# Delta-rule chunks of a gated delta net: four heads in flight with two PSUM banks each, levels confined to half of the columns, and one set of four tiles for scratch and levels

## The reference, cut to what matters

```python
k_beta = k * beta[..., None]
a_strict = jnp.where(idx[:, None] > idx[None, :],
                     jnp.einsum('bhncd,bhnsd->bhncs', k_beta, k) * decay, 0.0)
tri = a_strict + jnp.eye(c, dtype=jnp.float32)
u = lax.linalg.triangular_solve(tri, v * beta[..., None], left_side=True, lower=True, unit_diagonal=True)
w = lax.linalg.triangular_solve(tri, k_beta * jnp.exp(gc)[..., None], left_side=True, lower=True,
                                unit_diagonal=True)
qk = jnp.einsum('bhncd,bhnsd->bhncs', q, k) * decay
q_dec = q * jnp.exp(gc)[..., None]
k_dec = k * jnp.exp(g_last - gc)[..., None]
```

## Time and profile before

| what | value |
|---|---|
| median of 3 runs | 2913.43 us (2912.21 to 2916.68) |
| profiled execution | 2917.37 us, span 2915.6 us |
| mean granted clock in it | 0.92 |
| PE busy in the span | 2500.4 us (86%) |
| `stage_gdn_chunks`, first weight load to end of the last copy | 274.17 to 540.82 us |

### The profile page before, as it was taken

The page is one execution under the profiler, slowest core; times in us unless marked ns, Lnnn a source line. Parts: engine busy times, 40 slices in busy tenths (PEclk is TensorE's granted clock), DMA queues, the critical chain, the costliest instruction groups (busy, mean ns, idle before and its releaser), DMA issues. The chain is left out here.

```text
span 2915.6 us, 34741 instructions
## 1 busy us (share of the span) xinstructions
PE 2500.4 (86%) x13054; PEld 1953.1 (67%) x13054; DVE 1265.9 (43%) x2608; ACT 978.3 (34%) x1577; POOL 742.8 (25%) x204
## 2 busy tenths in 40 slices
PE   6996788877995696899799388979999888989998
PEld 4773777756773485567677265857887746768886
DVE  3533555445545323776554536143222453243122
ACT  2333111223552111673455225152322333343222
POOL 2430000042343231001334220413543301324441
PEclk8997889977997796999899698999999999999999
DMA  4251000015885233111688331213432302223321
GB/s 107 90 209 41 1 1 1 30 45 168 277 281 184 65 101 118 64 39 45 218 282 280 131 90 38 94 54 96 131 100 72 109 27 66 81 84 102 103 85 65
DMA packets 225098, 304.41 MB, mean 104 GB/s; under 512 B 52304, under 2 KB 139872, under 8 KB 224944
## 3 DMA queue, kind: packets, MB, share of 16 engines
q1 hardware_dynamic: 222656, 294.16, 31.3%
q0 software_dynamic: 2304, 8.39, 0.8%
HBM read 270.95 MB, written 31.56 MB: 104 GB/s over the span
## 5 line engine op out<-in xcount | busy, mean ns | idle before, releaser
L159 POOL TENSOR_TENSOR branch_weights_wl<-branch_weights_wf,branch_weights_wh 128x2048 fp32r<-128x2048 f32 (+1 forms) x66 | 303.9, 4604 | 770.2 <-ACT branch_weights_wh L153 770.2
L153 ACT ACTIVATE branch_weights_wh<-branch_weights_wf 128x2048 fp32r<-128x2048 f32 (+1 forms) x66 | 125.0, 1895 | 405.8 <-PE bprojc_acc L201 133.0
L201 PE MATMUL merge_acc<-xh,branch_weights_wh 128*128 128x512 f32 x384 | 151.4, 394 | 2.9 <-PEq L72 2.9
L201 PE MATMUL merge_acc<-xh,branch_weights_wl 128*128 128x512 f32 x384 | 150.3, 391 | 0.0
L201 PE MATMUL merge_acc<-xl,branch_weights_wh 128*128 128x512 f32 x384 | 149.5, 389 | 0.0
L159 POOL TENSOR_TENSOR nsa_weights_wl<-nsa_weights_wf,nsa_weights_wh 128x2048 fp32r<-128x2048 f32 x13 | 59.7, 4594 | 275.3 <-ACT nsa_weights_wh L153 275.3
L1556 PE MATMUL exp_ps_y<-rt_wf,exp_ht 128*128 128x512 f32 x256 | 117.2, 601 | 3.9 <-ACT exp_ht L1600 3.9
L1410 POOL TENSOR_TENSOR rt_wl<-rt_wf,rt_wh 128x2048 fp32r<-128x2048 f32 x16 | 82.6, 5163 | 128.9 <-ACT rt_wh L1406 128.9
L159 POOL TENSOR_TENSOR in_weights_wl<-in_weights_wf,in_weights_wh 128x2048 fp32r<-128x2048 f32 x16 | 75.3, 4709 | 129.1 <-ACT in_weights_wh L153 110.6
L201 PE MATMUL gproj_acc<-xh,in_weights_wh 128*128 128x512 f32 x256 | 100.8, 394 | 3.7 <-POOL in_weights_wl L159 3.7
L201 PE MATMUL gproj_acc<-xh,in_weights_wl 128*128 128x512 f32 x256 | 100.5, 393 | 0.0
(11 more groups left out here) (612 smaller groups left out, 6705.0 us busy)
## 6 DMA issues: line engine op xcount, KB each, us to landing
branch_weights_wf<-w_in SPq DMA_DIRECT2D x56, 1024.0 KB, 5.0
rt_wf<-moe_w_down SPq DMA_DIRECT2D x32, 1024.0 KB, 5.5
in_weights_wf<-gdn_w_in SPq DMA_DIRECT2D x16, 1024.0 KB, 5.6
rt_wf<-moe_w_gate SPq DMA_DIRECT2D x32, 512.0 KB, 7.4
rt_wf<-moe_w_up SPq DMA_DIRECT2D x32, 512.0 KB, 8.2
moe_rows<-rt_y SPq DMA_DIRECT2D x64, 256.0 KB, 2.1
moe_rows<-gproj_zeros SPq DMA_DIRECT2D x1, 12288.0 KB, 35.7
merge_bwf<-w_branch SPq DMA_DIRECT2D x12, 1024.0 KB, 5.0
```

The source lines that it names most:

```text
L153: act.activation(self.h[u][:, :, 0:self.cols(b)], self.s.f[u][:, :, 0:self.cols(b)], ACT.Copy).then_inc(self.s.hi_ready, 1)
L159: pool.tensor_tensor(self.l[u][:, :, 0:self.cols(b)], self.s.f[u][:, :, 0:self.cols(b)], self.h[u][:, :, 0:self.cols(b)].bitcast(F32), ALU ...
L201: mm = pe.matmul(self.acc[:, s, 0:cols], lhs[:, P * s:P * s + P], rhs, start=(u == 0 and k == 0 and n == 0), stop=(u == 1 and k == HALF - ...
```

## The change

`NB` is 4: two rounds of four heads. A head has two PSUM banks in place of four, and four SBUF tiles (`at`, `x`, `tm`, `um`) in place of ten, each used for several things in turn. The masks of levels 1 to 6 are transposed, so that the mask is laid on the product instead of on `at`. In a level only the half of the columns that can be nonzero is computed: `off` takes half of the columns of `tm` (64 of 128 per chunk, in runs of the block size) and writes them into the same half of the bank, DVE multiplies the whole bank with the mask into `x`, and `grow` makes two products of 64 columns, `um` with half of `x` and `x` with half of `um`, written side by side in bank 1. DVE subtracts these 256 columns each from the matching halves of `tm` and `um`. ACT's copy in the level is gone. Turning of keys and values moves from the start of a round to behind the levels, and with it its scaling; there ACT does both scalings and copies out the new keys.

```diff
+    NB, L = 4, LEVELS - 1
-        NB = 2
-        B = [{x: st.sb(f"{x}{i}", [P, TT, P]) for x in
-              ("dec", "decb", "eg", "at", "m", "x", "tm", "um", "kbg", "vb")} for i in range(NB)]
-        ps = [st.ps(f"ps{i}", 4) for i in range(NB)]
+        B = [{x: st.sb(f"{x}{i}", [P, TT, P]) for x in ("at", "x", "tm", "um")} for i in range(NB)]
+        ps = [st.ps(f"ps{i}", 2) for i in range(NB)]
...
+        def halves(ap, lv, e):
+
+            return ap.rearrange("p (b e s) -> p b e s", e=2, s=1 << lv)[:, :, e, :]
...
+                def off(i, r, lv):
+
+                    dve_did.wait(pe, i, r, "lower" if lv == 1 else f"lower{lv - 1}")
                     for c in range(TT):
+                        mm = pe.matmul(halves(bank(i, 0, c), lv, 0), B[i]["at"][:, c, :], halves(B[i]["tm"][:, c, :], lv, 0),
                                        start=True, stop=True)
...
+                def grow(i, r, lv):
...
+                    dve_did.wait(pe, i, r, f"off{lv}")
+                    if lv < L:
+                        for c in range(TT):
+                            pe.matmul(compact(ps[i][:, 1, 64 * c:64 * c + 64], lv), b["um"][:, c, :],
+                                      halves(b["x"][:, c, :], lv, 0), start=True, stop=True)
...
+                        mm = pe.matmul(compact(ps[i][:, 1, 256 + 64 * c:256 + 64 * c + 64], lv), b["x"][:, c, :],
+                                       halves(b["um"][:, c, :], lv, 1), start=True, stop=True)
+                    pe_did.done(mm, i)
...
+                def off(i, r, lv):
+                    pe_did.wait(dve, i, r, f"off{lv}")
+                    dve_did.done(dve.tensor_tensor(B[i]["x"][:], wide(ps[i][:, 0, :]), spread(levels[:, lv, :]), ALU.mult), i)
+
+                def grow(i, r, lv):
...
+                    pe_did.wait(dve, i, r, f"grow{lv}")
+                    if lv < L:
+                        low = chunk_halves(b["tm"][:], lv, 0)
+                        dve_did.done(dve.tensor_tensor(low, low, compact(ps[i][:, 1, 0:256], lv), ALU.subtract), i)
+                    up = chunk_halves(b["um"][:], lv, 1)
+                    dve_did.done(dve.tensor_tensor(up, up, compact(ps[i][:, 1, 256:512], lv), ALU.subtract), i)
...
+    lev[1:] = lev[1:].transpose(0, 2, 1)
```

More of the change, by code:

```diff
@@ L564, in stage_gdn_chunks @@
         ld = st.sem("loaded")
[L565 to L571, removed]
+        pe_did = Steps([st.sem(f"pe_done{i}") for i in range(NB)],
+                       ["decay", "gram", "beta", "score", "first"]
+                       + [f"{x}{lv}" for lv in range(1, L + 1) for x in ("off", "grow")]
+                       + ["turn_k", "turn_v", "new_v", "new_k"])
@@ L572, in flat, with wide @@
+        act_did = Steps([st.sem(f"act_done{i}") for i in range(NB)], ["growth", "decay", "k_beta", "v_beta", "new_k"])
+        dve_did = Steps([st.sem(f"dve_done{i}") for i in range(NB)],
+                        ["mask", "dec_beta", "at", "score", "query", "first", "upper", "lower"]
+                        + [f"{x}{lv}" for lv in range(1, L + 1) for x in (("off", "lower", "upper") if lv < L else ("off", "upper"))]
+                        + ["k_dec", "new_v"])
         def flat(ap):
             return ap.rearrange("p c n -> p (c n)")
+        def wide(ap):
+            return ap.rearrange("p (c n) -> p c n", c=TT)
@@ L655, in _ @@
                 for r in range(GDN_H // NB):
                     for i in range(NB):
-                        front(NB * r + i, i, r)
+                        decay(NB * r + i, i, r)
+                        gram(NB * r + i, i, r)
                     for i in range(NB):
-                        first_level(NB * r + i, i, r)
+                        beta(NB * r + i, i, r)
+                    for i in range(NB):
+                        score(NB * r + i, i, r)
+                    for i in range(NB):
+                        first(i, r)
@@ L660, in _ @@
                     for lv in range(1, L + 1):
                         for i in range(NB):
[L662 removed]
+                            off(i, r, lv)
                         for i in range(NB):
[L664 removed]
+                            grow(i, r, lv)
                     for i in range(NB):
[L666 removed]
+                        turned(NB * r + i, i, r)
+                    for i in range(NB):
+                        new(i, r)
@@ new lines, in turned, with new @@
+                    act_did.done(ins, i)
+                    pe_did.wait(act, i, r, "turn_v")
+                    for c in range(TT):
+                        col = GDN_H * c + h
+                        ins = act.activation(B[i]["tm"][:, c, :], ps[i][:, 1, P * c:P * c + P], ACT.Copy,
+                                             scale=gt["beta"][:, col:col + 1])
+                    act_did.done(ins, i)
+                def new(h, i, r):
+                    pe_did.wait(act, i, r, "new_k")
+                    act_did.done(act.activation(qkvz[:, GDN_H + h, :], ps[i][:, 0, :], ACT.Copy), i)
@@ L787, in _ @@
+                        for i in range(NB):
+                            grow(i, r, lv)
                     for i in range(NB):
-                        back(NB * r + i, i, r)
+                        k_dec_rows(NB * r + i, i, r)
+                    for i in range(NB):
+                        new(NB * r + i, i, r)
 def stage_gdn_scan(g, a, qkvz, gt, qk_t, k_dec):
```

212 lines of the change are left out of this document (99 added, 113 removed).

## The result

The changed kernel takes 2965.80 us (median of 4 runs, 2962.65 to 2966.70) against 2913.56 us before (2912.21 to 2916.68): a ratio of 1.0164, 95% interval 1.0151 to 1.0177. The profiled execution took 2965.82 us.

What follows compares the result with a forecast made beforehand. PE bounds the stage, each record costing its weight load. Two rounds of start 24.9, levels 115.9 and end 12.0, plus 2.0 and 1.2, give 308.8 us against 266.65, hence 2956 us; range 2886 to 2972.

Steps and rivals of the forecast that it cites:

- Column halves save nothing on PE: Levels: halving the streamed columns leaves a record at its weight load's price, 0.1115 us at full clock, 0.213 at half.
- The clock falls in the start: Start of every round: PE has 0.89 us of work every 2.55 us for 10 us, so its clock falls.
- 64 columns do not bring it back: Levels: the 64-column stream stays at clock 0.50, records costing 0.213 in place of 0.1115 us, 55 us a round.
- The choice of the end: Levels: 64-column records taken to act on the clock like 20 to 40 columns, since weight loads space them too.
- The sum: Stage: start 24.9, levels 115.9, end 12.0, a round 152.8; two rounds with 2.0 and 1.2 added make 308.8 us.
- The ends: End of a round, turning and new rows: 11.5 us at full clock with ACT's last scaling, 12.0 in the sum.
- the 3.9 us taken off: Whole kernel: 2959.6 us for the profiled execution lowered to 2956, as the profiled execution before lay 3.9 above the median.
- What four heads gain: Stage: four heads gain about 66 us in waits, some 50 us of it given back by the starts of rounds.
- The clock that holds: Rival, levels: the clock holds or returns at once, stage 200 us, -66, kernel 2847; chance 0.13.
- Cheap short records: Rival, levels: short records cost under 0.1 us at full clock, DVE bounds, stage 149 us, kernel 2796; chance 0.04.
- Slow gapped columns: Rival, levels: columns with gaps cost 0.268 us a record, stage 371 us at full clock, kernel 3017; chance 0.03.
- The break-even: Levels: the change becomes faster once more than 38% of level records run at full clock, undoing 42 of 110 us.

Runs made afterwards that it cites:

- wide_level_1: The change with 128 streamed columns in level 1 alone, 64 in levels 2 to 6; 2853.23 us, ratio 0.9781 to the kernel before.
- half_weights: The change with repeated transposing matmuls at round starts, its level matmuls taking 64 weight columns and streaming 128, output unusable; 2850.87 us, ratio 0.9757 to before.
- busy_first: The change with the first step's four transposing matmuls issued twice for the first three heads of a round; 2850.13 us, ratio 0.9770 to before.
- interleaved: The change with level 1's first products placed between the heads' transposing products and streaming 128 columns; 2849.85 us, ratio 0.9760 to before.
- wide_levels: The change with every level matmul streaming all 128 columns again, DVE still subtracting only halves; 2856.13 us, ratio 0.9780 to the kernel before.
- two_heads_wide_1: The change with two heads in flight in place of four and 128 columns in level 1; 2871.07 us, ratio 0.9823 to the kernel before.
- two_heads: The change with two heads in flight in place of four, levels still streaming 64 columns; 2972.45 us, ratio 1.0182 to the kernel before.

## Why the prediction was right

**Column halves save nothing on PE.** Right in its effect: 0.1117 us a record at full clock (wide_level_1; 0.1115 forecast) and 0.213 at half, in every level. The reason given, "a record costs what its weight load costs", holds only where the load is the longer side. half_weights shows the other bound, the stream, at the same 0.11 us. The rows read then (40 and 20 columns against 128 weights) could not show it.

**The clock falls in the start.** Right: PE idles 1.56 us ahead of three of the four `first` groups, which stand 2.53 us apart (2.55 forecast), and the clock falls in the window 298 to 302. busy_first shows by removal that this start is the cause, in all its runs; interleaved agrees in the one execution that was profiled.

**64 columns do not bring it back.** Right, and it was the forecast's weakest step, since no row of before was 64 columns wide for long. The choice of the end was argued from the spacing of the records, which the rows don't settle: records of 128 columns are as far apart (0.1117 us in wide_levels) and do bring the clock back. So there was luck in it. Measured: 116 us of records without a gap stayed at 0.50, twice. wide_levels and wide_level_1 show by replacement that 128 columns do bring it back, within some 4 us. What the prediction had not separated is that the same 64-column stream keeps 1.00 once it has it; that is why one wide level is enough.

**The sum.** The start of the second round is 455.31 - 430.42 = 24.9 us (24.9 forecast); the first, with the cold beginning and the masks' DMA, 301.42 - 274.39 = 27.0 (26.9). The levels are 417.37 - 301.42 = 115.95 us (115.9). The ends are the term that was mis-sized: 430.42 - 417.37 = 13.1 us for the first (12.0 forecast), and 13.8 with the last copy (13.2), although the wait of 0.8 us for ACT that the forecast held did not come (no load from 417.37 to 430.42 has a bracket): the records ran at half clock up to about 422, 5 us, and the forecast had put 0.5 us to that. The stage is 310.7 us, 1.9 above the forecast.

The median is 9.8 us above the 2956 forecast. Besides those 1.9 us, the other stages took 4.1 us more from the end of this stage on (2378.9 against 2374.8; 2377.6 to 2387.1 in the experiments with a shorter stage). And the 3.9 us taken off, because the profiled execution of before lay that far above its median, had no counterpart: after's profiled execution lies at its median. Why the later stages differ by some microseconds from kernel to kernel, though their code is the same, was not tried.

**What four heads gain.** The prediction put down about 66 us to the waits that four heads fill. The saving at full clock is near in size: 266.65 - 195.3 = 71.4 us in busy_first, with 266.65 - 200 = 66 forecast. The start's share in it was put too high, since the 25.4 us of the first round, which begins at half clock, was taken for all four; the second round's start takes 22.3. And the cause of the saving was put in the wrong place: of the 70.3 us that wide_level_1 saves, 53.6 come with two heads (two_heads_wide_1), from the shorter chain in a level and the rewritten start and end, and 16.7 from four heads in flight.

**The rivals.** The clock that holds was forecast at 2847 for the change; busy_first, in which it holds, takes 2850.13. The price of that case was right and its condition was not met. Cheap short records fall with 0.1117 us a record for 64 columns at full clock. Slow gapped columns fall with runs of 2 as fast as runs of 64, at either clock. The break-even (38% of the level records at full clock) was not tried; two_heads, with one of four rounds at full clock, is still slower than before.

## What to carry to other kernels

Before narrowing matmuls, look at which side sets the record's price: here halving the stream alone saved nothing, halving both sides halved the record. Then look at the clock on either side of the edit: a narrow stream can look fully busy for a hundred microseconds at 0.50, so "PE busy" must be read with PEclk beside it. Where a stretch has gaps and narrow work follows, leave the first narrow step wide, which cost next to nothing here and was worth 114 us of the stage. Filling the gaps with work that is already there (the next step of another head) kept the clock too, but it was tried only together with a wide first product.

## What the runs showed of the hardware

- The granted clock has a memory: the same 64-column stream ran at 1.00 for all of levels 2 to 6 in wide_level_1 and at 0.50 for 116 us in the change. PE was busy throughout in both. The Trainium skill's page "TensorE: Matmul & The Clock Gate", section "What's actually happening", says that the default state is throttled and that activity releases the throttle; these traces agree for 128 columns (back within some 4 us in wide_levels) and differ for 64 (0.50 for 116 us with PE busy throughout), where the measurement decides.
- An fp32 record costs the longer of load and stream: 0.112 us (128 weight columns, 64 streamed), 0.109 (64, 128), 0.112 (128, 128), 0.058 (64, 64), all at full clock.
- A start with two gaps of 1.56 us lost the clock in three rounds of one execution (two_heads) and kept it in the second of the four, with the same instructions and gaps; with four groups in a row (the change, wide_levels, wide_level_1) it was lost in both rounds of each profiled execution.
